# Nine of 48 weight transfers, each split by partitions into 120 and 8

## The reference, cut to what matters

```python
def block(x_blk):                                  # 128 tokens
    qry = (x_blk @ w_query).reshape(T, 8, 2, 128)
    scores = einsum('thpd,hpnd->thpn', qry, sub_keys)
    ...                                            # top 16 of 16 x 16 pairs, per head
    u = expert_u[idx]                              # 128 experts for each token
    act = gelu(einsum('thkd,td->thk', u, x_blk), approximate=False)
    vsel = expert_v[idx]
    return einsum('thk,thkd->td', gate * act, vsel)
...
h = h + mix; h = h + peer(rmsnorm(h, norm_ffn[i]), ...)
return rmsnorm(h, norm_final)
```

## Time and profile before

| | us |
|---|---|
| median of 3 runs | 1578.97 |
| lowest and highest | 1577.9, 1581.96 |
| the profiled execution's own time | 1579.55 |
| its span, first to last instruction | 1577.5 |
| PE busy | 1362.1 (86%) |
| DVE busy | 975.1 (62%) |
| ACT busy | 670.4 (42%) |
| POOL busy | 580.3 (37%) |

### The profile page before, as it was taken

One profiled execution on the slowest core, in us unless ns is written; L12 is line 12 of the kernel. 1 busy time (PEld: TensorE's weight loads), 2 busy tenths in 40 slices (PEclk: granted clock), 3 DMA queues, 4 the chain that ended last, 5 costly groups with the idle time before them and its releaser, 6 DMA issues.

```text
span 1577.5 us, 15019 instructions
## 1 busy us (share of the span) xinstructions
PE 1362.1 (86%) x4096; PEld 656.8 (42%) x4096; DVE 975.1 (62%) x2432; ACT 670.4 (42%) x1914; POOL 580.3 (37%) x532
## 2 busy tenths in 40 slices
PE   7999998889877988889989699888999877787776
PEld 5555565444323433334555244334465422222222
DVE  3327598988774344764477765566556888554544
ACT  2324443434334334873434333586433434443433
POOL 1001565554443333443433234334434433333330
PEclk9999999999998999999999799999999999999999
DMA  9317999999999999999999999999999999999995
GB/s 380 146 54 293 396 413 421 421 421 421 421 421 422 421 421 421 421 421 421 421 421 421 372 422 421 421 413 399 421 421 420 421 421 421 422 422 422 421 421 230
DMA packets 85234, 620.42 MB, mean 393 GB/s; under 512 B 10368, under 2 KB 10368, under 8 KB 11424
## 3 DMA queue, kind: packets, MB, share of 16 engines
q0 software_dynamic: 74768, 551.65, 84.4%
q1 hardware_dynamic: 9792, 67.51, 10.5%
q10 hardware_dynamic: 592, 0.31, 0.1%
HBM read 618.38 MB, written 1.05 MB: 393 GB/s over the span
## 4 chain that ended last, share of the span: by engine, by line
PE 40%; DMA 37%; DVE 9%; ACT 9%; issue 4%; POOL 1%; SPq 0%; ACTq 0%; DVEq 0%; POOLq 0%
PE banks L533 25%; DMA arena<-in_peer_uv_dram,hnT 24%; PE banks L560 6%; PE banks L413 5%; DMA work<-in_peer_uv_dram,hnT 5%; DMA raw<-in_peer_uv_dram,hnT 4%; DVE arena L1413 3%; DMA rt<-in_diff_lambda_k_dram 2%; ACT g_e L917 2%; PE banks L681 2%; DMA spare<-in_peer_uv_dram,hnT 2%; ACT L954 1%; PE banks L505 1%; ACT hnT L909 1%; DVE raw L1413 1%
## 5 line engine op out<-in xcount | busy, mean ns | idle before, releaser
L533 PE MATMUL banks<-arena,g_e 128*128 128x512 f32 x1184 | 585.1, 622 | 116.1 <-ACT g_e L917 115.0
L339 POOL DMA_INDIRECT arena<-in_peer_uv_dram,hnT x299 | 326.3, 1091 | 515.8 <-PE banks L533 497.8
L533 PEld LDWEIGHTS banks<-arena,g_e 128*128 128x128 f32 x1184 | 214.3, 195 | 405.5 <-ACT g_e L917 213.2
L906 ACT ACTIVATE hnT<-hnT 128x1 f32<-128x1 f32 x512 | 103.3, 202 | 631.5 <-DVE hnT L1413 629.6
L1413 DVE CUSTOM_DVE_ANT_0 arena<-arena,hrows 128x1024 f32<-128x1024 f32 x209 | 254.2, 1223 | 170.2 <-DMA arena<-in_peer_uv_dram,hnT 168.9
L533 PE MATMUL banks<-raw,g_e 128*128 128x512 f32 x424 | 205.5, 611 | 27.8 <-ACT g_e L917 25.3
L917 ACT ACTIVATE g_e<-ident,hnT 128x128 f32<-128x128 f32 x501 | 201.2, 402 | 46.5 <-ACT hnT L909 0.7
L339 POOL DMA_INDIRECT raw<-in_peer_uv_dram,hnT x106 | 118.3, 1116 | 154.1 <-PE banks L533 149.5
L909 ACT ACTIVATE hnT<-hnT,arena 128x1 f32<-128x1 f32 x512 | 150.7, 294 | 52.1 <-DVE arena L1594 5.5
L1413 DVE CUSTOM_DVE_ANT_0 arena<-arena,banks 128x1024 f32<-128x1024 f32 x90 | 109.7, 1220 | 87.3 <-DMA arena<-in_peer_uv_dram,hnT 87.2
L1413 DVE CUSTOM_DVE_ANT_0 raw<-raw,hrows 128x1024 f32<-128x1024 f32 x80 | 97.6, 1224 | 57.2 <-DMA raw<-in_peer_uv_dram,hnT 56.3
(11 more groups left out here) (244 smaller groups left out, 1259.2 us busy)
## 6 DMA issues: line engine op xcount, KB each, us to landing
arena<-in_diff_in_dram SPq DMA_DIRECT2D x24, 1024.0 KB
arena<-in_peer_query_dram SPq DMA_DIRECT2D x16, 1024.0 KB
arena<-in_gla_in_dram POOLq DMA_DIRECT2D x5, 2048.0 KB, 20.3
arena<-in_peer_query_dram SPq DMA_DIRECT2D x4, 2048.0 KB, 10.9
arena<-in_diff_out_dram SPq DMA_DIRECT2D x8, 1024.0 KB
arena<-in_peer_uv_dram,hnT POOLq DMA_INDIRECT x299
work<-in_gla_out_dram POOLq DMA_DIRECT2D x2, 2048.0 KB, 40.0
arena<-in_gla_in_dram SPq DMA_DIRECT2D x2, 1024.0 KB, 12.3
```

Source lines behind the costliest of these rows:

```text
L339: pool.indirect_dma_start(pair(n), None, table, bass.IndirectOffsetOnAxis(ap=places[:, o:o + 1].bitcast(u32), axis=0)).then_inc(S(f"pair_l ...
L533: last = nc.tensor.matmul(bank(2 * (tile % NT) + half), diags[:, slot * P:(slot + 1) * P], v_row(n)[:, half * 512:(half + 1) * 512], start ...
L906: A(acts[:, o:o + 1], dots[:, o:o + 1], ACT.Gelu).then_inc(S("gelu_done"), 1)
```

## The change

Nine of the 48 halves, n = 3, 9, 15, 21, 27, 32, 37, 42 and 47, are loaded in two transfers: one over partitions 0 to 119 (960 KB) that raises `half_loaded`, and one over partitions 120 to 127 (64 KB) that raises a new semaphore, `rest_loaded`. PE waits for both before it uses such a half. The same bytes go to the same places, and the other 39 halves are loaded as before.

```diff
+MOST = 120
+PARTED = (3, 9, 15, 21, 27, 32, 37, 42, 47)
...
-                    sp.dma_start(ar(A_HALF[n % 4], WBLK // 2), w[j // 2][:, c0:c0 + WBLK // 2]
-                                 ).then_inc(S(f"half_loaded{n % 4}"), 16)
+                    place, half = ar(A_HALF[n % 4], WBLK // 2), w[j // 2][:, c0:c0 + WBLK // 2]
+                    if n in PARTED:
+                        sp.dma_start(place[0:MOST, :], half[0:MOST, :]).then_inc(S(f"half_loaded{n % 4}"), 16)
+                        sp.dma_start(place[MOST:P, :], half[MOST:P, :]).then_inc(S("rest_loaded"), 16)
+                    else:
+                        sp.dma_start(place, half).then_inc(S(f"half_loaded{n % 4}"), 16)
...  in block1:
                         pe.wait_ge(S(f"half_loaded{halves % 4}"), 16 * (halves // 4 + 1))
+                        if halves in PARTED:
+                            pe.wait_ge(S("rest_loaded"), 16 * (PARTED.index(halves) + 1))
...  in query1:
                     pe.wait_ge(S(f"half_loaded{(halves + j) % 4}"), 16 * ((halves + j) // 4 + 1))
+                    if halves + j in PARTED:
+                        pe.wait_ge(S("rest_loaded"), 16 * (PARTED.index(halves + j) + 1))
```

## The result

The changed kernel takes 1621.07 us (median of 4 runs, 1619.57 to 1621.69) against 1578.72 us: 42.35 us more, a ratio of 1.0267 with a 95% interval of 1.0255 to 1.028. The forecast was 1575.1 us in a range of 1570 to 1593. The sign and the size were wrong.

The account below looks back on a forecast made before the run. Full DMA engines, paced by the slowest, were taken as the bound. From the profiled 1579.55 us, - 3.5 - 1.75 + 1.4 gave 1575.7; less 0.58 to the median, 1575.1 us, range 1570 to 1593.

Parts of the forecast that it names:

- What bounds the kernel: Over the whole span: the 16 DMA engines are full at 421 GB/s, and the slowest engine sets the pace.
- It takes load from one engine: In nine parted halves: 120 rows fill 15 engines, leaving one engine 22.4 us less work.
- If the engine left out is the last: At the span's end: the spared engine is the last straggler, so the end waits for the next-last, 3.5 us less.
- the whole gain of 3.5 + 1.75 us: Relieving the last engine saves 3.5 us at the span's end and 1.75 us at the end of tile 0.
- the rival with a chance of 0.10: At the end: the last engine is one of the eight given 2.8 us more, nothing is relieved; 1581.8 us.
- Collisions: In parted halves: engines writing the same SBUF part slow packets, 10 to 23 us; 1589 to 1602 us, chance 0.24.
- Issues and waits: SP's nine more issues, 4 us in all, and PE's second wait are covered and cost nothing.
- The landing estimate of 8 us: A parted half and its rest land within 8 us, against 18 us between issue and use by PE.
- Nothing shifted: Rows go over all sixteen engines, or the spared engine ends early: 1579.0 us, chance 0.13.
- the rest lands late: At PE's waits for parted halves: nine waits of some 2.8 us cost 25 us; 1604 us, chance 0.03.
- The landing at the end of tile 0: The landing at 878.20 that holds the chain at tile 0's end should come a little before 878.

Follow-up runs that it names:

- the two separate runs: Against the kernel before, nine halves: one loaded only partitions 0 to 119, 1609.36 us; the other loaded whole halves, then rows 120 to 127 again, 1591.71 us.

## Why the prediction was wrong

**What bounds the kernel** was right: the DMA engines are full, the slowest sets the pace, and no cover hid a loss of rate. Each microsecond that the packets took longer is in the time. (POOL's step is 2.49 us by the earlier trace rows, not 2.48, which changes nothing.)

**"It takes load from one engine"** was right as to what the transfer does: 15 and 8 engines, by the 63 packets. The Trainium skill, "DMA: Bandwidth & Descriptors", in its part on how many engines a transfer uses, states this rule, and the trace agrees.

**"If the engine left out is the last"** is the first of two steps of the forecast that failed, and the one behind its sign. It carried the whole gain of 3.5 + 1.75 us, and nothing in the rows spoke for it: the earlier trace rows show that one engine is late and not which. The runs put the last one among the second to fourth of the engines, where it isn't spared but given eight-row work, 2.8 us. This was the rival with a chance of 0.10, which by itself gives 1581.8 us. The same page of the Trainium skill says that engines 7 and 15 are usually slower than the rest. In this kernel the last one is neither, if the engines are counted from 0 and small transfers use the lowest-numbered, as the Trainium skill has it there and no run here shows: it is then 1, 2 or 3, and the measurement decides.

**Collisions** are the second step, and nearly the whole loss: the sum has no term for them, so the forecast put the price of a parted half at nothing. The prediction named the mechanism, its place and its signature rightly, but as a rival at a chance of 0.24 and a size of 10 to 23 us. There too the price was too low: 1.1 to 2.6 us for a parted half, 4.7 us measured (3.4 for the 120 rows, 1.5 for the eight, by the two separate runs). The range of prices came from rows at a restart of dry queues, a disturbance of another cause, and it took a half's 1 MB as the only thing slowed down. The windows around half 15 show what it left out: the expert steps share the disturbed parts, and two thirds of the added engine time is theirs (25.6 of 39.7 us). The eight rows are small but bad: 64 KB cost 1.5 us, of which only 0.3 are their own work.

**How the engines meet** is shown for the eight rows as far as the place: it is where rows are written in the SBUF. For the 120 rows, the larger share of the loss, it is carried over from them; what was shown there is that every cut by partitions costs and the cut by columns doesn't. That the parts are groups of four partitions, each with its own engine in a 128-row transfer, fits all runs: spaced by four, eight rows of eight engines cost 3.6 us; the top eight, which are two such groups, 13.3. An estimate bears it out: the top eight add four packets of 0.311 us to each of their two groups, 4 x 0.311 x 9 = 11.2 us, the spaced eight one packet to each, 2.8 us. The Trainium skill, "SBUF — State Buffer", in its section on the DMA port swizzle, gives a map of 16 ports, with two groups of four partitions on each. By it the top eight partitions lie on two ports, the spaced eight on eight. The runs agree (13.3 and 12.2 us against 3.6 and 2.8). How the packets of the 120 rows lie on the engines, in blocks of eight or otherwise, no run showed directly.

**Issues and waits** at nothing: right, by the cut by columns (1.2 us). The landing estimate of 8 us was too short: the large parts took 13 to 18 us, those of `diff_in` 16.6 against their cover of 18.

**Nothing shifted** and **the rest lands late** did not come about. The landing at the end of tile 0, put a little before 878, came at 901: the losses of the parted halves before it had added up.

Behind both steps lies the order of the chances. The gain needed an engine to be the right one of sixteen; the loss needed only that a transfer be laid out otherwise than the one shape of which the trace showed that it runs undisturbed.

## What to carry to other kernels

When a window shows the DMA engines full, look at GB/s beside the share: a full share at a lower rate means that packets are slower, and here the whole of it came out in the time. Load over all 128 partitions and cut by columns if a transfer has to be cut; here that cost 1 us where each cut by partitions cost 29 to 42. To learn whether an engine has slack, give it extra work in a size that can be measured, before moving work away from it.

## What the runs showed of the hardware that was not expected

An engine beside the straggler can take 14.9 us of added work over the span at no cost (0.9996, 0.9986 to 1.0005), although the mean share of the engines is 1.01 in nearly every window. The slack shows in the few stretches where the engines run dry. From 880 to 930 us the share is 0.96 before, 0.98 with one row more for each half and 0.92 with four. The likely account is that engines ahead of the straggler stand still there and catch up their added work; the traces don't name the engines, so it is not shown.

Reloading 15 or 16 rows at a stride of eight partitions costs 34 us, 19 more than four to eight rows at a stride of four, though each engine still does one row. By the reading above these rows don't lie on their own engine's group. If groups 32 partitions apart share a part, as the prediction weighed, they lie two to a part, and a part gets 2 x 14.9 = 29.9 us of added work, an estimate near the 34 measured; it was not tested apart.
